# Activations with tokens on the partitions in a two-layer attention and MLP trunk, and attention heads placed between projection chunks

## What is computed

```python
for l in range(DEPTH):                                   # 2 layers
    h = rms_norm(x, attn_norm[l])
    z = h @ w_in[l]                                      # 2048 -> 512+256+64+512+512+1024+16+1024
    z_cq, z_ckv, z_kr, z_q, z_k, z_v, z_a, z_g = split_cols(z, IN_SPLITS)
    q  = rms_norm(z_cq, cq_norm) @ w_uq                  # 8 heads of 128 + 64 (rotary)
    kv = rms_norm(z_ckv, ckv_norm) @ w_ukv               # 8 heads of 128 (k) and 128 (v)
    ...                                                  # RMS norm of q and k per head, rotary part,
    a_out = softmax(q k' * scale, mask by chunks of 64) v   # then an RMS norm over all heads
    ...
    state = state * decay + k_dec' v ; o = q state       # gated linear attention, 4 chunks, 4 heads
    g_out = rms_norm(o) * silu(z_g)
    x = x + concat(a_out, g_out) @ w_out[l]              # 2048 -> 2048
    h = rms_norm(x, ffn_norm[l])
    u = causal_dwconv(h @ w_up[l])                       # 2048 -> 11264, width 3 along the tokens
    x = x + (silu(gate) * up) @ w_down[l]                # 5632 -> 2048
```

## Time and profile before

| | |
|---|---|
| median of three runs | 2262.56 us |
| the profiled execution | 2264.97 us |
| its span, first to last instruction | 2263.1 us |
| what lies around the span | 1.9 us |
| mean granted TensorE clock | 0.99 of full |
| moved from memory | 390.3 MB, 173 GB/s over the span |

### The profile page before, as it was taken

How to read it: one execution, slowest core, us unless ns; L and a number is a source line. 1 busy time by engine, 2 the same in 40 slices (tenths; PEclk the granted TensorE clock), 3 DMA queues, 4 the chain that set the end, 5 groups by cost and what they waited for, 6 DMA issues and landing times.

```text
span 2263.1 us, 29736 instructions
## 1 busy us (share of the span) xinstructions
PE 2216.6 (98%) x12490; PEld 1911.9 (84%) x12490; DVE 1764.4 (78%) x2180; ACT 1003.3 (44%) x974; POOL 105.9 (5%) x68
## 2 busy tenths in 40 slices
PE   7999998999999999999999999899999999999998
PEld 6888787888888888888878888688888888888887
DVE  5557967787888887788965588678887788888779
ACT  4434544444433344433545264454444444334444
POOL 2000203000000000000010010120000000000001
PEclk9999999999999999999999999899999999999999
DMA  5654434555555555655555445255555555565564
GB/s 194 194 160 137 141 114 131 186 186 186 186 189 195 194 185 186 204 186 187 186 174 175 132 134 158 81 166 192 197 182 188 192 186 187 191 199 186 186 198 137
DMA packets 330457, 394.32 MB, mean 174 GB/s; under 512 B 14672, under 2 KB 269428, under 8 KB 330068
## 3 DMA queue, kind: packets, MB, share of 16 engines
q1 hardware_dynamic: 330100, 392.09, 53.2%
q0 software_dynamic: 224, 0.33, 0.1%
HBM read 390.30 MB, written 2.10 MB: 173 GB/s over the span
## 4 chain that ended last, share of the span: by engine, by line
PE 89%; DVE 8%; ACT 1%; issue 1%; DMA 0%; POOL 0%; SPq 0%; DVEq 0%; ACTq 0%
PE G L1314 32%; PE X L1314 20%; PE G L1315 16%; PE X L1315 10%; DVE lo L859 2%; PE G L1418 2%; PE G L1420 2%; PE G L1419 2%; DVE xT L872 1%; DVE xT L870 1%; DVE hx L888 1%; PE X L1429 1%; PE X L1440 1%; PE X L1637 1%; PE X L1567 0%
## 5 line engine op out<-in xcount | busy, mean ns | idle before, releaser
L859 DVE TENSOR_TENSOR lo<-raw,hi 128x2048 fp32r<-128x2048 f32 (+1 forms) x366 | 831.2, 2274 | 164.0 <-ACT hi L576 159.1
L576 ACT ACTIVATE hi<-raw 128x2048 fp32r<-128x2048 f32 (+1 forms) x366 | 695.5, 1902 | 583.2 <-PE G L1315 313.2
L1314 PE MATMUL G<-hx,hi 128*128 128x512 f32 x2496 | 882.4, 398 | 3.2 <-DVE hx L1275 3.2
L1315 PE MATMUL G<-hx,lo 128*128 128x256 f32 x2496 | 695.6, 279 | 0.0
L1314 PEld LDWEIGHTS G<-hx,hi 128*128 128x128 f32 x2496 | 469.6, 188 | 118.3 <-issue 4.3
L1314 PE MATMUL X<-hx,hi 128*128 128x512 f32 (+1 forms) x1440 | 500.4, 394 | 0.0
L1315 PEld LDWEIGHTS G<-hx,lo 128*128 128x128 f32 x2496 | 470.8, 189 | 0.7
L1315 PE MATMUL X<-hx,lo 128*128 128x256 f32 (+1 forms) x1440 | 399.0, 277 | 0.0
L1314 PEld LDWEIGHTS X<-hx,hi 128*128 128x128 f32 (+1 forms) x1440 | 268.7, 187 | 63.8
L1314 PE MATMUL G<-mid,hi 128*128 128x512 f32 x832 | 293.6, 396 | 0.4 <-DVE qkn L864 0.4
L1315 PEld LDWEIGHTS X<-hx,lo 128*128 128x128 f32 (+1 forms) x1440 | 269.0, 187 | 0.0
(11 more groups left out here) (210 smaller groups left out, 1898.9 us busy)
## 6 DMA issues: line engine op xcount, KB each, us to landing
raw<-in_w_up SPq DMA_DIRECT2D x176, 1024.0 KB, 5.1
raw<-in_w_down SPq DMA_DIRECT2D x88, 1024.0 KB, 5.1
raw<-in_w_in SPq DMA_DIRECT2D x62, 1024.0 KB, 5.2
raw<-in_w_out SPq DMA_DIRECT2D x32, 1024.0 KB, 5.4
raw<-in_w_uq SPq DMA_DIRECT2D x8, 768.0 KB, 4.8
raw<-in_w_ukv SPq DMA_DIRECT2D x4, 1024.0 KB, 5.7
z<-in_x SPq DMA_DIRECT2D x1, 1024.0 KB, 4.9
qkn<-in_x SPq DMA_DIRECT2D x1, 1024.0 KB, 7.0
```

The lines of the kernel that those rows point to most:

```text
L576: act.activation(hi[:, k % SLOTS, 0:n], raw[:, k % SLOTS, 0:n], ACT.Copy).then_inc(hi_ready, 1)
L859: dve.tensor_tensor(lo[:, s, 0:n], raw[:, s, 0:n], hi[:, s, 0:n].bitcast(F32), ALU.subtract).then_inc(lo_ready, 1)
L1314: pe.matmul(bank, w_hi, x2, start=first, stop=False)
L1315: return pe.matmul(bank[:, T:2 * T], w_lo, x2[:, 0:T], start=False, stop=last)
```

## The change

Everything but `w_up` is computed with x stationary and the weights streaming. x is held as `xk`, tokens on the partitions, as it is in memory, and is turned for each norm (`turn_x`, 32 transposes twice a layer); the copy out of PSUM takes the gain and the rounding. Sums over features come from ACT (`Square` with an accumulated sum). The latent c, q, k, the gated q, the outputs of both mixers are turned by transposes. `w_down` and `w_out` are added to x with one instruction per 128 x 512. The output is stored from `xk`.

The order is new: cq, kv with the gate rank, k of the gated part, `ukv`, q of the gated part, `uq`, v, g, `w_out` (the a half first), MLP. The eight heads stand between half chunks of v and g (`filler`). The gated linear attention comes after the heads.

Cut to what the text below speaks of. PE, where `bank_free(l, un)` waits until unit `un - 2` has been copied out, and `updates(n0)` alternates between rows 0 to 63 and 64 to 127:

```diff
+            def tokens_pass(bank, x2, b, w_hi, w_lo, first, last):
+                x_hi, x_lo = x2[:, b * P:(b + 1) * P], x2[:, T + b * P:T + (b + 1) * P]
+                pe.matmul(bank, x_hi, w_hi, start=first, stop=False)
+                pe.matmul(bank, x_lo, w_hi, start=False, stop=False)
+                return pe.matmul(bank, x_hi, w_lo, start=False, stop=last)
...
+            def turn_x(l, which, q):
+                wait_x(pe, l, which, q)
...
+                for n in range(2):
+                    for j in range(2):
+                        tile = 4 * q + 2 * n + j
+                        for b in range(TT):
+                            mm = pe.transpose(banks[:, n, j * T + b * P:j * T + (b + 1) * P], xk[:, b, tile * P:(tile + 1) * P], ident)
+                    mm.then_inc(x_turned.sem, 1)
...
+                for j in range(2):
+                    w_hi, w_lo = take(l, K_UKV + j)
+                    for side in range(2):
+                        un = U_UKV + 2 * j + side
+                        bank_free(l, un)
...
+                        if side == 0:
+                            mm.then_inc(unit_half.sem, 1)
+                    mm.then_inc(slot_free, 1)
...
+                for p in range(4):
+                    scores(p)
+                    filler(4 * p)
+                    filler(4 * p + 1)
+                    turn_probs(2 * p)
+                    filler(4 * p + 2)
+                    values(2 * p)
+                    turn_probs(2 * p + 1)
+                    filler(4 * p + 3)
+                    values(2 * p + 1)
...
+                for n in range(17, 21):
+                    filler(n)
...
+                pe.wait_ge(a_ready.sem, a_ready.at(l, HEADS))
...
+                updates(0)
+                for n in range(21, 24):
+                    filler(n)
...
+                reads(0)
+                reads(1)
...
+                out_chunk(38)
...
+                updates(2)
+                out_chunk(39)
+                out_chunk(40)
...
+                reads(2)
+                reads(3)
+                out_chunk(41)
+                out_chunk(42)
+                for i in range(4):
+                    if i == 0:
+                        pe.wait_ge(o_gated.sem, o_gated.at(l, 8))
...
```

DVE. `copy_kraw(j)` copies unit 3 + 2j and so frees the banks of unit 5 + 2j:

```diff
+                split(l, 14)
+                by_token(U_GK, K_GK + 3, gk)
...
+                split(l, 15)
+                copy_kraw(0)
...
+                split(l, 16)
+                copy_kraw(1)
...
+                split(l, 22)
+                q_out(1)
+                q_rope(1)
...
+                    find_top(2 * p)
+                    find_top(2 * p + 1)
+                    split(l, k + 2)
+                    if p >= 1:
+                        copy_values(2 * p - 1)
...
+                for h in range(HEADS):
+                    if h == 6:
+                        split(l, 38)
...
+                split(l, 39)
+                state_step(0)
+                state_step(1)
...
+                split(l, 42)
+                state_step(2)
+                state_step(3)
+                gate_o(0)
+                split(l, 43)
+                add_to_x_when_done(l, U_OUT + 1, a_rs)
+                copy_o(1)
+                split(l, 44)
+                gate_o(1)
...
-                dve.tensor_tensor(two, bank2(u)[:, :, 0:T], two, ALU.add).then_inc(x_added, 1)
-                dve.wait_ge(x_added, l * X_ADDS + n + 1)
-                dve.tensor_tensor(two, bank2(u)[:, :, T:2 * T], two, ALU.add).then_inc(unit_free, 1)
...
+                        ins = dve.tensor_tensor(x, bank2(u + q)[:, b, :], x, ALU.add)
```

ACT, with `a_square(h)` waiting for `copy_values(h)` and `o_square(1)` for `copy_o(1)`:

```diff
+                for p in range(4):
+                    k = K_GV + 4 + 2 * p
+                    split(l, k + 2)
+                    if p >= 1:
+                        a_square(2 * p - 1)
+                    exps(2 * p)
+                    exps(2 * p + 1)
+                    split(l, k + 3)
...
+                split(l, 43)
+                o_square(1)
+                split(l, 44)
...
```

More of the change, by code:

```diff
@@ new lines, in _ @@
+                tokens(l, K_GV, C_GV)
+                tokens(l, K_GV + 4, C_GV + 512)
+                tokens(l, K_G, C_G)
+                tokens(l, K_G + 4, C_G + 512)
+                for part in range(2):
+                    for q in range(4):
+                        for c in range(2):
+                            load(l, K_OUT + 8 * part + 2 * q + c, (4, 512),
+                                 w_out[l, :, 8 * part + 4 * c:8 * part + 4 * c + 4, 512 * q:512 * q + 512])
+                mlp_order(l, up, down)
@@ L953, in up, with add_to_x_when_done, down @@
                     gated_product(l, g, 1)
-                    mid_round_off(l, g, par, 1)
-            def down(l, g, par, r, k, ur, u):
+                    mid_round_off(l, g, 1)
+            def add_to_x_when_done(l, u, factor=None):
+                dve.wait_ge(slot_free, done(l, K_OUT + 2 * (u - U_OUT) + 1))
+                add_to_x(l, u, factor)
+            def down(l, g, k, u):
+                last = g + 1 == NG
                 for q in range(4):
-                    if k + q + 2 <= CHUNKS:
-                        split(r, k + q + 2)
-                    if q == 0 and k + 4 < CHUNKS:
+                    if l * CHUNKS + k + q + 2 < DEPTH * CHUNKS:
+                        split(l, k + q + 2)
+                    if q == 0 and not last:
@@ L1305, in _, with take @@
+                split(l, 46)
+                split(l, 47)
+                add_to_x_when_done(l, U_OUT + 3, a_rs)
+                split(l, 48)
+                split(l, 49)
+                for q in range(3):
+                    add_to_x_when_done(l, U_OUT + 4 + q)
+                    split(l, 50 + 2 * q)
+                    split(l, 51 + 2 * q)
+                    x_low(l, 1, q)
+                mlp_order(l, up, down)
         @block.tensor
         def _(pe):
-            def take(r, k):
-                pe.wait_ge(lo_ready, r * SLOTS + (k + 1 + SLOTS))
+            def take(l, k):
+                pe.wait_ge(lo_ready, done(l, k))
@@ L1695, in shape_constants @@
+                for k in range(43, 46):
+                    out_chunk(k)
+                for k in range(46, 54):
+                    pe.wait_ge(o_ready.sem, o_ready.at(l, 4 if k == 46 else 8))
+                    out_chunk(k)
+                    if k in (48, 50, 52):
+                        turn_x(l, 1, (k - 48) // 2)
+                mlp_order(l, up, down)
 def shape_constants():
```

2173 lines of the change are left out of this document (1062 added, 1111 removed).

## The result

The changed kernel takes 2252.45 us, the median of 20 runs from 2248.94 to 2256.66. The kernel before, run on the same chip in turn with it, takes 2275.47 us (20 runs, 2262.26 to 2293.11). The ratio is 0.990, with an interval of 0.9876 to 0.9924. The prediction was 2247 us, 2222 to 2288, "within 1%" the likeliest case. The time fits, but not every term of the sum does: some came out too small and others too large, and most of that cancels.

A forecast was written before the change was run, and what follows sets the result against it. PE's work plus its waits was taken as the bound. Attention 399.7, MLP 733.0, attention 381.4, MLP 729.7 and tail 3.9 sum to a 2247.7 us span; after small adjustments the forecast was 2247 us, range 2222 to 2288.

The forecast's parts named there:

- within 1%: Whole kernel: the case of a time neither below 2240 us nor above 2285 us, given 0.53.
- The price of a product: Chunks on PE: 24 matmuls of 0.227 us, 5.45 us a chunk with x stationary, against 5.55 in the old form.
- The pair: `w_up` in the MLP: old-form matmul pairs at 0.3468 us each, 88 chunks taking 488.3 us.
- PE's work in attention: Each attention stage: PE's work falls from 366 to 336.9 us, streaming 282.1, float32 46.1, changes of kind 8.7.
- the rival with dearer transposes: All 300 new or moved transposes cost twice 0.11 us, 33 us more, 2280 us; 7%. The skill's figure: 55 us more.
- The waits: Attention stages: PE waits 36.4 us a layer, where it waited 12.4, for copies standing behind splits.
- the gate of o: After chunk 41 in attention: 12.1 us of additions, copies, squares, splits and gate leave PE waiting 6.7 us.
- The clock: Behind attention's waits: half clock costs 2.2 us for each of three long waits, 1.5 for one shorter; 8.1 a layer.
- The start: Layer 0: a quarter of x and one chunk suffice, so PE's first chunk starts near 12 us instead of 20.0.
- The tail: Kernel end: one addition, hops and the store take 3.9 us after the last product, instead of 15.0.
- The updates: State updates in attention: 16 matmuls on alternating row halves at 0.29 us each, 4.6 us for 7.7; other end 7.7.
- The faster rival: DVE reaches the copies before splits block it; no waits at `ukv` or gate of o, 51 us less, 2196 us; 15%.

The follow-up runs named there:

- e_warm: Changed kernel with overwritten 512-column float32 matmuls keeping PE busy in the three long waits of each layer; 2242.33 us.
- b_tail: Kernel before without the leftover work for a third layer (loads, splits, squares, parts of x) in its last layer; 2270.2 us, ratio 0.9986.
- e_rows: Changed kernel with four state updates in a row on the same half of the rows instead of alternating halves; 2263.54 us.
- e_kraw: Changed kernel with the copies of the `ukv` stage (gated k, raw keys, v) put ahead of the splits; 2222.84 us.
- e_gate: Changed kernel with `copy_o(1)` directly after `gate_o(0)`, and `gate_o(1)` ahead of the addition of chunk 41 and `split(44)`; 2237.83 us.
- e_all: Changed kernel with the moves of e_kraw, e_gate and e_start, plus low parts of a and state steps ahead of the splits; 2185.48 us.
- e_start: Changed kernel with the small parameter loads on POOL's queue held back until the last quarter of x has landed; 2251.53 us.
- e_best: e_all with one overwritten 8-column matmul ahead of each of the 18 `w_up` groups that follow a `w_down` group; 2172.24 us.
- e_short: e_all with overwritten short matmuls of 8 to 512 columns ahead of 14 of the 18 `w_up` groups that follow `w_down`; 2184.0 us, single execution.
- b_short: Kernel before with one overwritten 8-column matmul behind the sums of squares in each MLP stage; 2276.64 us.

## Why the prediction was right, and where it wasn't

| | predicted | measured |
|---|---|---|
| attention of layer 0 ends | 399.7 | 396.9 |
| MLP of layer 0 | 733.0 | 739.6 |
| attention of layer 1 | 381.4 | 374.1 |
| MLP of layer 1 | 729.7 | 737.1 |
| from the last product to the end | 3.9 | 3.3 |

- **The price of a product.** With x stationary a matmul takes 0.227 us as said (96 in 21.8). The pair was the failed step: "0.3468 us each" came from the earlier trace rows, a profile in which both MLP stages happened to run at the shorter of two periods. In after 9 of 11 groups run at 0.3532: 9 x 128 x 0.0065 = 7.5 us a stage, which is the whole error of the stage of layer 1 (7.4) and of that of layer 0 (6.6). One profile didn't show that there was a second value. The runs did hint at it: 2276.93 stood beside 2262.4.
- **PE's work in attention.** 374.1 less 32.0 of waits and 8.0 of clock (both below) is 334.1 us; predicted 336.9. The reads are part of the difference, 0.35 us each at full clock for 0.43, and the updates another, 0.24 for 0.29. The transposes cost 0.11 us at full clock, as read from the earlier trace rows (16 in 1.7 us). This answers the rival with dearer transposes, but not by the clock it quotes: the 0.95 of the earlier trace rows counts the time ahead of the first clock entry, at 14.4 us, as full speed. Up to there the transposes start 0.21 us apart, half clock:

```profile
13.75 0.42 PE L1387 MATMUL G<-cst,qkn 128*128 128x128 f32 x1
13.96 0.42 PE L1387 MATMUL G<-cst,z 128*128 128x128 f32 x1
...
14.52 0.27 PE L1387 MATMUL G<-cst,qkn 128*128 128x128 f32 x1
14.63 0.27 PE L1387 MATMUL G<-cst,z 128*128 128x128 f32 x1
```

  The distance falls to 0.11 at 14.4, after 5.6 us in which PE ran nothing but transposes; so they don't keep the clock down. The 55 us of that rival is also a slip, 300 x (0.275 - 0.11) is 50.
- **The waits.** 32.0 us a layer for 36.4. Right within 0.2 us at `ukv` (12.0 for 12.2) and within 0.7 at a, the reads and `uq`. Too long were the heads (2.8 for 4.8) and the gate of o (5.6 for 6.7), both sums over many short steps of two engines.
- **The clock.** 8.1 us a layer predicted, 9.5 in layer 0 and 8.0 in layer 1 measured. This is what matmuls take above their time at full clock: full chunks 4.6 and 4.8, updates 1.7 and 1.5, reads 1.5 and nothing, the 16 transposes of o 1.7 in each. A long wait costs 2.0 us (e_warm) where 2.2 was taken. A shorter wait that brings it down was expected too; it is the one of 2.5 us before the updates, in layer 0 also one of 2.3 before the reads.
- **Attention as a whole.** Layer 1 came out 7.3 us below the sum: 4.4 of it waits, 2.8 PE's work, the clock nearly nothing.
- **The start.** The first chunk came at 17.2 us, not at 12: the first quarter of x landed at 8.7. The error of 5 us at the first chunk was 3.4 at the end of the gated k (82.7 for 79.3; how it shrank I did not follow), and the shorter waits made up for it.
- **The tail** was right, 3.3 us for 3.9, and for the reason given (b_tail).
- **The updates.** 0.24 us for 0.29 at full clock. But two of the four groups ran at half clock, 3.5 us each, which came to more than the gain. The other end of the range would have been 0.43, not 0.48, and even the order of e_rows gives 0.36. The rule of the Trainium skill (TensorE: Matmul & The Clock Gate, Part 3: Packing small matmuls) on row groups agrees in direction: 1.93 against 2.9 us. The trace shows more than an overlapping weight load: the two matmuls themselves start 0.007 us apart.
- **The faster rival**, 2196 us, was no account of this kernel, since the lists do block; but its sum says what the order costs: e_kraw and e_gate, which take away the waits at `ukv` and at the gate, gain 29.6 and 14.6 us, 44 where it said 51.

The terms that failed were +14 us (pairs), -7 (attention of layer 1) and -3 (layer 0); their sum, with 0.6 less at the end, is 3 us of a span. Another 2 us come from the 2.4 taken off for the profiled execution, which in after lies only 0.4 above the median. That the total was 5 us off, and its largest error 14, is luck: nothing in the runs ties the period of the pairs to the waits that made up for it. Measured against the lowest level of before, from which the prediction was made, the change brings 10 us where 16 were forecast.

## What to carry to other kernels

In a list of an engine that works in order, put the copy that frees a bank ahead of the split that waits for the chunk just finished: the split has chunks of slack, the copy has none, and here the two orders differ by 66 us of 2252 (e_all without the 1 us of e_start), three times what the new layout brought by the medians. Price each wait of some microseconds with the clock behind it. And when runs of one kernel lie in levels, take a profile of each level before a duration from one of them goes into a sum that has thousands of it.

## What the runs showed of the hardware that I had not expected

- The same stream of pairs (a matmul of 512 columns, then one of 256) has two exact periods, 0.3467 and 0.3533 us, at a granted clock of 1.00, and keeps the one it begins with through 128 to 2080 pairs. In the new kernel what precedes it settles which. Behind stretches of `w_down` (512-column matmuls in threes) it was the longer one in all 130 groups of eight traces; with one matmul of 8 columns between them the shorter in all 19 (e_best, e_short). One group each in e_short had the shorter with 16 or 32 columns or with two matmuls of 64 or of 128, and the longer with one of 64 or more columns. In the kernel before the same program gets the one or the other from execution to execution, and a short matmul there changes nothing (b_short). What the two values are in the machine stays open.
- A wait of 5.6 us costs 2.0 us more through the clock (1.4 to 2.8 at six places, e_warm against after); one of 2.5 us ahead of eight small float32 matmuls 0.9 to 1.7 us (2.85 to 3.60 for 1.93, in the traces of after, e_kraw, e_gate and e_warm). Behind waits of 2.0 to 2.3 us the clock fell in some places and not in others, with the same instructions.
- Float32 matmuls with 64 rows each, on different halves of the rows, run side by side: they start 0.007 us apart and two take 0.43 us together, as long as one.
- A stretch of nothing but transposes, 5.6 us long and 0.21 us apart, ended at full clock, with 0.11 us between starts (before, 8.8 to 15 us).
- With small loads beside the first large ones 44 GB/s were moved between 3 and 5 us, where 157 were without them, and still x was delayed by no more than 1.1 us (after against e_start).
